# The low parts of the weights move from VectorE to GpSimd

## The chip, the cores and the metric

The kernel runs on one core of a Trainium2 chip. The metric is the device time of one execution in microseconds (us), as the median of the timed runs. The engines of the core are TensorE (PE, with its weight loads as PEld), VectorE (DVE), ScalarE (ACT), GpSimd (POOL) and SyncE (SP). Each runs its own program; they meet at semaphores.

## The reference

Two blocks of transformer-like layers run one after the other on one sequence of 512 tokens with 1024 channels, all in float32:

```python
def first_block(x, ...):
    for layer in range(DEPTH):                      # DEPTH = 2
        if layer % 2 == 0:
            x = x + even_mixer(rms_norm(x, even_norm[i]), even_w_in[i], even_w_out[i])
        else:
            x = x + diff_mixer(rms_norm(x, odd_norm[i]), odd_w_qkv[i], ...)
        x = x + conv_ffn(rms_norm(x, ffn_norm[layer]), ffn_w_up[layer], ..., ffn_w_down[layer])
    return rms_norm(x, final_norm)

def second_block(x, ...):
    for l in range(DEPTH):
        proj = x @ w_in[l]                          # retention, mLSTM and gates
        ...
        mix = (gate_a * y_ret + gate_b * y_ml) @ w_out[l]
        x = _layer_norm(DEEPNORM_ALPHA * x + mix, ln1_g[l], ln1_b[l])
        gu = x @ w_gate_up[l]
        hidden = jax.nn.silu(gu[..., :D_FF_2]) * gu[..., D_FF_2:]
        x = _layer_norm(DEEPNORM_ALPHA * x + hidden @ w_down[l], ln2_g[l], ln2_b[l])
    return x
```

Nearly all of the work is products of the activations with weight matrices. What matters here is that they must come out more exact than one pass of TensorE's fast float32 format (fp32r) gives.

## The kernel before

**Products in three passes.** Each weight w is split into a high part (w_hi, w rounded to fp32r) and a low part (w_lo = w - w_hi), and each activation likewise (h_hi, h_lo and others). A product is the sum of high by high, high by low and low by high, three matmuls of 512 columns for each weight tile of 128x128.

**Units.** The weights lie in memory as 512 units, in the order in which PE uses them. A unit is mostly 128x1024 float32 (four weight tiles of 256 columns, or two of 512); 16 units are half as large. A unit has 24 matmuls on PE. For each unit four engines do one thing: SP loads it into one of RAW = 3 raw buffers (w_raw); ACT makes w_hi in one of HL = 4 buffers; DVE makes w_lo in one of 4 buffers; PE multiplies. ACT waits until PE has finished the unit four before; SP waits until w_hi and w_lo of the unit three before are made, since they are read from the same raw buffer.

**Order.** There is no scheduler. Each engine's program is written out by hand and walks through the products in the same order with a class Panels, whose loops (fm for products with features in the rows, tm and tm_in_halves for products with tokens in the rows) call next_unit() wherever the next unit begins. On ACT and DVE next_unit() splits units up to HL ahead of the one that PE begins, so an engine's own work (copies, norms, attention) and the splits stand in one fixed order. On DVE the split of a unit is line L1423. Around it stand:

- L1546, L1817: h_lo of the norms. L1810, L1793: the layer norm's tiles; in layer_norm a call of next_unit() stands at the third tile.
- L1740, L1753, L1773, L1758: the convolution taps and the hidden tiles of the feed-forward blocks.
- L1598, L1626 (or L1623, L1624), L1633, L1725: the attention's score reduction with its row minimum, the normalising of probabilities, a copy of transposed probabilities, and a half of the copies of v out of PSUM. The other half is ACT's, L1098.

**Attention beside a product.** In both attentions of the first block the product for v (L574 on PE, tm_in_halves) is mixed with the steps of the first heads: scores (L640), transposes (L649), values (L660). This product uses two PSUM banks over and over, so it stops until DVE and ACT have copied v out. DVE's call there is `walk.tm_in_halves(beside_values(steps), late=True)`, which puts the unit's split behind the attention steps and ahead of the next copy of v.

**GpSimd before** (pool_program) does little: it starts table loads at certain points of the program, raises the head sums of the second attention to the power -0.5 (L2119), and helps with two tiles in the last norm (L2131, L2135).

**Once**: every wait goes through it; it leaves out a wait on a value that this engine has already seen.

Of the kernel before, what the change touches and what calls it, by code (L numbers as in the profile page):

```python
# [18 lines left out]
DT = D // P  # L19
TB = S // P  # L20
D_FF = 2816
FT = D_FF // P
# [96 lines left out]
RAW, HL = 3, 4  # L119
# [10 lines left out]
UNITS = weight_units()  # L130
# [1281 lines left out]
def dve_program(e, fl, m):  # L1412
    w = Once(e)
    mark, after, bank, scr, stats = fl.mark, fl.after, m.bank, m.scr, m.stats
    at = {"unit": 0, "split": 0}
    swapped = []

    def split_unit():
        u = at["split"]
        if u < N_UNITS:  # L1420
            n = UNITS[u][3] * UNITS[u][5]
            w.wait_ge(*after("w_hi", u))
            e.tensor_tensor(m.w_lo[u % HL][:, 0:n], m.raw[u % RAW][:, 0:n], f32(m.w_hi[u % HL][:, 0:n]),  # L1423
                            ALU.subtract).then_inc(*mark("w_lo", u))
            at["split"] += 1

    def next_unit():
        while at["split"] < min(at["unit"] + HL, N_UNITS):
            split_unit()
        at["unit"] += 1  # L1430

    walk = Panels(next_unit)
# [358 lines left out]
    def layer_norm(st, gain, shift, split):  # L1791
# [13 lines left out]
        for f in range(DT + 1 if split else ON_POOL):  # L1805
            if f == 2:
                next_unit()
            if f < DT:
                w.wait_ge(*after("recentred", (st, f)))
                e.scalar_tensor_tensor(m.x[:, f, :], m.x[:, f, :], m.p(gain, f), bank[SPREAD][:, :],  # L1810
                                       ALU.mult, ALU.mult).then_inc(*mark("x_normed", (st, f)))
            if f + ahead < (DT if split else ON_POOL):
                recentre(f + ahead)
            if f and split:
                g = f - 1
                w.wait_ge(*after("h_hi", (st, g)))
                e.scalar_tensor_tensor(m.h_lo[:, g, :], m.x[:, g, :], m.p(shift, g), f32(m.h_hi[:, g, :]),  # L1817
                                       ALU.add, ALU.subtract).then_inc(*mark("h_lo", (st, g)))
# [195 lines left out]
    split_unit()  # L2014
    w.wait_ge(*after("gains_in", 0))
    for f in range(DT):
        low_part("e", f, "even_norm")
        if f in (2, 4):
            split_unit()
    for f in range(1, DT):  # L2020
        tally_square("e", f)
        if f == 3:
            split_unit()
# [12 lines left out]
    for f in range(DT + 1):  # L2036
        if f == 2:
            next_unit()
# [55 lines left out]
def pool_program(e, fl, m, params, tables):  # L2094
    w = Once(e)
    mark, after, scr = fl.mark, fl.after, m.scr
    gains = PARAMS["subln"][0]

    w.wait_ge(*after(f"x_in{X_ON_SP - 1}", 0))
# [5 lines left out]
    for n, st in enumerate("ed"):  # L2105
# [3 lines left out]
        rows = [table(tables, "mask_rows")[:, i * S:(i + 1) * S] for i in range(2)]  # L2109
        w.wait_ge(*after("sumsq", (st, 7)))  # L2110
        if st == "e":
            e.dma_start(scr[4][:, :], rows[0]).then_inc(*mark("mask_rows_in", 0, by=16))
            e.dma_start(scr[5][:, :], rows[1]).then_inc(*mark("mask_rows_in", 1, by=16))
        else:
            e.dma_start(m.tally[:, :], rows[0]).then_inc(*mark("mask_rows_in", 2, by=16))
            for f0, f1 in HEAD_BATCHES.values():
                inv_head = m.stats[:, 128 + TB * f0:128 + TB * f1]
                w.wait_ge(*after("head_sums", f1 - 1))
                e.tensor_tensor(inv_head, inv_head, m.eps[:, 2:3].to_broadcast([P, TB * (f1 - f0)]), ALU.pow).then_inc(*mark("head_inv", f0))  # L2119
    for layer in range(DEPTH):  # L2120
# [4 lines left out]
            *mark("tables_in", ("rope", L), ("decay", L), by=16))  # L2125
        w.wait_ge(*after("headnorm", ("r" + L, NH2 * TB - 1)))
        e.dma_start(m.select, table(tables, "select")[0:NH2, :]).then_inc(*mark("tables_in", "select" + L, by=16))
    last = f"r{DEPTH}"
# [212 lines left out]
```

## Time and profile before

| what | value |
|---|---|
| timed runs | 3097.36 us median of 3 (3097.26 to 3099.04) |
| profiled execution, whole | 3099.19 us |
| its span | 3097.4 us |
| TensorE (PE) busy | 3069.8 us, 99% |
| VectorE (DVE) busy | 1611.7 us, 52% |
| ScalarE (ACT) busy | 1133.8 us, 37% |
| GpSimd (POOL) busy | 20.5 us, 1% |
| HBM traffic | 89 GB/s over the span |

A busy time is the sum of an engine's instructions in one profiled execution. A PE that counts as busy for 99% means that its matmuls overlap without a gap that the profile can see nearly all the time; it is a modelled end that closes small gaps. For the other engines it is what they work.

### The profile page before, as it was taken

Reading aid. Unit: us, or ns where it says so; the run is one execution under the profiler, and the core shown is the slowest. Engines: PE = TensorE matmul, PEld = TensorE weight load, DVE = VectorE, ACT = ScalarE, POOL = GpSimd, SP = SyncE. Lnnn points to the kernel's source line nnn. Section 1 sums busy time; section 2 is a strip of 40 time slices with the busy share of each in tenths; the row PEclk is TensorE's granted clock in tenths of the full one; section 3 lists DMA queues with packets and bytes.
Section 4 is the critical chain, followed back from the end, with each engine's and each line's share of the span. In section 5 each row is a group of like instructions: output and inputs, shape, how many; then the busy total and the mean of one; then the engine's idle time right before and its main releaser. Section 6 shows DMA issues by size and latency. Waiting matters only on the chain.

```text
span 3097.4 us, 35265 instructions
## 1 busy us (share of the span) xinstructions
PE 3069.8 (99%) x14003; PEld 2478.0 (80%) x14003; DVE 1611.7 (52%) x2498; ACT 1133.8 (37%) x1765; POOL 20.5 (1%) x27
## 2 busy tenths in 40 slices
PE   9999999999999999999999999999999999999998
PEld 7668888886688888887888888888887888888887
DVE  6766775366567753664424463334674424453324
ACT  3454443224544432344323343222454323333222
POOL 0000000000000000000000000000000000000000
PEclk9999999999999999999999999999999999999999
DMA  6312222242122232412232223323412232323321
GB/s 200 96 35 96 95 96 102 95 140 74 35 96 96 96 102 95 136 57 80 79 98 90 95 89 95 102 93 105 130 55 68 89 96 89 95 95 96 95 96 68
DMA packets 86531, 289.56 MB, mean 93 GB/s; under 512 B 11448, under 2 KB 11448, under 8 KB 86112
## 3 DMA queue, kind: packets, MB, share of 16 engines
q1 hardware_dynamic: 84016, 279.75, 28.4%
q0 software_dynamic: 1488, 6.22, 0.6%
q8 instruction: 112, 1.84, 0.2%
q10 hardware_dynamic: 864, 1.33, 0.1%
q14 instruction: 51, 0.42, 0.0%
HBM read 272.58 MB, written 2.10 MB: 89 GB/s over the span
## 4 chain that ended last, share of the span: by engine, by line
PE 95%; DVE 3%; ACT 1%; issue 1%; DMA 0%; ACTq 0%; DVEq 0%
PE banks L482 75%; PE banks L547 6%; PE banks L512 3%; PE banks L574 2%; PE banks L640 1%; PE banks L660 1%; PE banks L818 1%; PE banks L838 1%; PE banks L439 1%; PE banks L649 1%; PE banks L852 1%; PE banks L613 1%; PE banks L929 0%; DMA x_resid<-x_fm 0%; PE banks L803 0%
## 5 line engine op out<-in xcount | busy, mean ns | idle before, releaser
L1423 DVE TENSOR_TENSOR w_lo<-w_raw,w_hi 128x1024 fp32r<-128x1024 f32 (+1 forms) x512 | 612.2, 1207 | 880.8 <-ACT w_hi L969 879.8
L969 ACT ACTIVATE w_hi<-w_raw 128x1024 fp32r<-128x1024 f32 (+1 forms) x512 | 526.7, 1040 | 790.8 <-PE banks L482 729.8
L482 PE MATMUL banks<-h_hi,w_hi 128*128 128x512 f32 x2304 | 712.6, 390 | 0.5 <-ACT h_hi L1312 0.5
L482 PE MATMUL banks<-h_lo,w_hi 128*128 128x512 f32 x2304 | 709.7, 389 | 0.1
L482 PE MATMUL banks<-h_hi,w_lo 128*128 128x512 f32 x2304 | 709.3, 389 | 0.0
L482 PEld LDWEIGHTS banks<-h_lo,w_hi 128*128 128x128 f32 x2304 | 432.3, 188 | 90.9 <-DVE h_lo L1546 0.8
L482 PEld LDWEIGHTS banks<-h_hi,w_lo 128*128 128x128 f32 x2304 | 432.4, 188 | 90.0
L482 PEld LDWEIGHTS banks<-h_hi,w_hi 128*128 128x128 f32 x2304 | 430.3, 188 | 91.7 <-issue 2.8
L482 PE MATMUL banks<-hid_hi,w_hi 128*128 128x512 f32 x668 | 206.4, 390 | 0.0
L482 PE MATMUL banks<-hid_lo,w_hi 128*128 128x512 f32 x668 | 205.7, 389 | 0.0
L482 PE MATMUL banks<-hid_hi,w_lo 128*128 128x512 f32 x668 | 205.6, 389 | 0.0
L482 PEld LDWEIGHTS banks<-hid_hi,w_hi 128*128 128x128 f32 x668 | 125.4, 188 | 26.8 <-issue 1.0
L482 PEld LDWEIGHTS banks<-hid_hi,w_lo 128*128 128x128 f32 x668 | 125.4, 188 | 26.1
L482 PEld LDWEIGHTS banks<-hid_lo,w_hi 128*128 128x128 f32 x668 | 125.4, 188 | 26.1
L1112 ACT ACTIVATE scratch<-scratch,params_sb 128x512 f32<-128x512 f32 x88 | 67.0, 809 | 173.1 <-DVE scratch L1753 173.1
L1740 DVE SCALAR_TENSOR_TENSOR scratch<-scratch,params_sb,scratch 128x510 f32<-128x510 f32 (+1 forms) x176 | 122.4, 748 | 12.6 <-ACT scratch L1112 12.6
L1108 ACT ACTIVATE hid_hi<-scratch 128x512 fp32r<-128x512 f32 x88 | 54.3, 633 | 165.7 <-DVE scratch L1787 105.4
L1753 DVE TENSOR_TENSOR scratch<-banks,inverse_rms 128x512 f32<-128x512 f32 x88 | 56.7, 686 | 89.5 <-PE banks L482 80.2
L547 PE MATMUL banks<-w_hi,h_hi 128*128 128x512 f32 x256 | 82.7, 404 | 0.0
L547 PE MATMUL banks<-w_hi,h_lo 128*128 128x512 f32 x256 | 79.2, 390 | 0.0
L547 PE MATMUL banks<-w_lo,h_hi 128*128 128x512 f32 x256 | 78.9, 389 | 0.0
L482 PE MATMUL banks<-z_hi,w_lo 128*128 128x512 f32 x256 | 78.8, 389 | 0.0
(300 smaller groups left out, 3358.9 us busy)
## 6 DMA issues: line engine op xcount, KB each, us to landing
w_raw<-weights SPq DMA_DIRECT2D x496, 512.0 KB, 3.6
scratch<-scratch SPq DMA_DIRECT2D x128, 64.0 KB, 2.0
w_raw<-weights SPq DMA_DIRECT2D x16, 256.0 KB, 2.5
scratch<-scratch SPq DMA_DIRECT2D x32, 128.0 KB, 2.3
decay<-tables POOLq DMA_DIRECT2D x2, 1024.0 KB, 5.9
y_fm<-x_resid SPq DMA_DIRECT2D x8, 256.0 KB, 2.2
x_resid<-x_fm ACTq DMA_DIRECT2D x5, 256.0 KB, 8.0
rope<-tables POOLq DMA_DIRECT2D x2, 512.0 KB, 4.0
```

The lines of the kernel that those rows point to most:

```text
L439: mm = e.matmul(bank[b][:, tokens], wt[:, k, j * P:(j + 1) * P], a[:, kt + k, tokens], start=bool(j) and kt + k == kt0 and step == 0, stop ...
L482: mm = e.matmul(bank[b][:, :], wt[:, k, j * P:(j + 1) * P], a[:, kt, :], start=kt == 0 and step == 0, stop=step == 2 and (kt == k_tiles - ...
L512: mm = e.matmul(bank[b][:, :], weight[u % HL][:, :].rearrange("p (k c) -> p k c", k=4)[:, k, j * P:(j + 1) * P], a[:, kt, :], start=kt == ...
L547: mm = e.matmul(bank[t][:, :], a[:, kt, t * P:(t + 1) * P], wt[:, k, :], start=kt == 0 and step == 0, stop=kt == DT - 1 and step == 2)
L574: mm = e.matmul(bank[b][:, :], a[:, kt, t * P:(t + 1) * P], wt, start=kt == 0 and step == 0, stop=kt == DT - 1 and step == 2)
L613: mm = e.matmul(bank[b][:, tb * P:(tb + 1) * P], every_column(m.stats[:, first + tb:first + tb + 1]), m.ident[:, :], start=tb == 0, stop=T ...
L969: e.activation(m.w_hi[u % HL][:, 0:n], m.raw[u % RAW][:, 0:n], ACT.Copy).then_inc(*mark("w_hi", u))
L1108: e.activation(m.hid_hi[int(tag)][:, f, :], scr[2 + f % 2][:, :], ACT.Copy).then_inc(*mark("hid_hi", (tag, f)))
L1112: e.activation(scr[t][:, :], scr[4 + f % 2][:, :], ACT.Identity, bias=m.p("fconv_b" + tag, channels), scale=m.p("fconv_w" + tag, 2 * 2 * F ...
L1423: e.tensor_tensor(m.w_lo[u % HL][:, 0:n], m.raw[u % RAW][:, 0:n], f32(m.w_hi[u % HL][:, 0:n]), ALU.subtract).then_inc(*mark("w_lo", u))
L1740: c = e.scalar_tensor_tensor(scr[t][:, back:S], scr[u][:, 0:S - back], m.p("fconv_w" + tag, (2 - back) * 2 * FT + channels), scr[t][:, bac ...
L1753: e.tensor_tensor(scr[4 + f % 2][:, :], bank[b][:, :], m.r_bc[:, :], ALU.mult).then_inc(*mark(flow, (tag, f)))
```

## The change

The splits of all 512 units into low parts leave DVE's program and go to GpSimd's. DVE's walk keeps its loops, but with nothing to do where a unit begins. GpSimd gets a walk of its own, which passes through all the products in order with the helpers through and through_tm; its old work (table loads, head sums) stands between the stretches of that walk. The subtraction itself, its operands and its marks are the same. ACT, PE and SP are not changed, and PE and SP now wait for GpSimd's w_lo where they waited for DVE's.

```diff
 def dve_program(e, fl, m):
...
-    def split_unit():
-        u = at["split"]
-        if u < N_UNITS:
-            n = UNITS[u][3] * UNITS[u][5]
-            w.wait_ge(*after("w_hi", u))
-            e.tensor_tensor(m.w_lo[u % HL][:, 0:n], m.raw[u % RAW][:, 0:n], f32(m.w_hi[u % HL][:, 0:n]),
-                            ALU.subtract).then_inc(*mark("w_lo", u))
-            at["split"] += 1
-
-    def next_unit():
-        while at["split"] < min(at["unit"] + HL, N_UNITS):
-            split_unit()
-        at["unit"] += 1
-
-    walk = Panels(next_unit)
+    walk = Panels(lambda: None)
...
         for f in range(DT + 1 if split else ON_POOL):
-            if f == 2:
-                next_unit()
...
-    split_unit()
     w.wait_ge(*after("gains_in", 0))
     for f in range(DT):
         low_part("e", f, "even_norm")
-        if f in (2, 4):
-            split_unit()
...
 def pool_program(e, fl, m, params, tables):
...
+    at = {"unit": 0, "split": 0}
+
+    def split_unit():
...
+    def next_unit():
...
+    walk = Panels(next_unit)
+
+    def through(tiles, k_tiles):
+        for _ in walk.fm(tiles, k_tiles):
+            pass
+
+    def through_tm():
+        for _ in walk.tm(iter(())):
+            pass
+
+    for _ in range(2):
+        split_unit()
     w.wait_ge(*after(f"x_in{X_ON_SP - 1}", 0))
     e.dma_start(m.ones[:, :], table(tables, "ones")).then_inc(*mark("small_in", 0, by=16))
...
+        next_panel = walk.fm(DT, DT)
+        next(next_panel)
         w.wait_ge(*after("sumsq", (st, 7)))
...
+        for _ in next_panel:
+            pass
+        through(DT, DT)
+        through_tm()
+        if st == "d":
             for f0, f1 in HEAD_BATCHES.values():
                 inv_head = m.stats[:, 128 + TB * f0:128 + TB * f1]
                 w.wait_ge(*after("head_sums", f1 - 1))
                 e.tensor_tensor(inv_head, inv_head, m.eps[:, 2:3].to_broadcast([P, TB * (f1 - f0)]), ALU.pow).then_inc(*mark("head_inv", f0))
+        through(DT, DT)
+        through(2 * FT, DT)
+        through(DT, FT)
...
+        through(DT, DT)
+        through_tm()
+        through(DT, DT)
         w.wait_ge(*after("headnorm", ("r" + L, NH2 * TB - 1)))
         e.dma_start(m.select, table(tables, "select")[0:NH2, :]).then_inc(*mark("tables_in", "select" + L, by=16))
+        through_tm()
+        for _ in range(7):
+            through(DT, DT)
+        through(2 * FT, DT)
+        through(DT, FT)
```

The first place is DVE's program beside the v product of the second attention, at the second of its four copies of v. Before, a low part stands ahead of the copy of v (L1725):

```order
L1598 ISA prob_d,stats<-banks,diagonals 128x256
L1598 ISA stats 128x1
L1633 COPY probt_d<-banks 128x384
L1626 SCALAR_TENSOR_TENSOR prob_d<-prob_d,stats 128x256
L1423 TENSOR_TENSOR w_lo_61<-w_raw_54,w_hi_57 128x1024
L1725 TENSOR_SCALAR v_d<-banks,stats 128x512
L1598 ISA prob_d,stats<-banks,diagonals 128x128
```

With the change the same piece reads (line numbers are 16 lower):

```order
L1582 ISA prob_d,stats<-banks,diagonals 128x256
L1582 ISA stats 128x1
L1617 COPY probt_d<-banks 128x384
L1610 SCALAR_TENSOR_TENSOR prob_d<-prob_d,stats 128x256
L1709 TENSOR_SCALAR v_d<-banks,stats 128x512
L1582 ISA prob_d,stats<-banks,diagonals 128x128
```

The copy of v has moved up behind the normalising of the probabilities; the rest is as it was. The same happens wherever L1423 stood, 512 times.

The second place is the beginning of GpSimd's program. Before, it goes from the memsets to the loads of tables:

```order
L2100 DMA ones<-tables 128x128
L2101 DMA ident<-tables 128x128
L2102 DMA eps<-tables 128x3
L2103 DMA params_sb<-params 128x1369
L2104 DMA masks_f_77<-tables 128x768
L2108 DMA rope_e<-tables 128x1024
L2112 DMA scratch_73<-tables 128x512
```

With the change (the numbers tell the buffers of a ring apart):

```order
L2080 ISA
L2080 TENSOR_TENSOR w_lo_59<-w_raw_52,w_hi_55 128x1024
L2080 TENSOR_TENSOR w_lo_60<-w_raw_53,w_hi_56 128x1024
L2102 DMA ones<-tables 128x128
L2103 DMA ident<-tables 128x128
L2104 DMA eps<-tables 128x3
L2105 DMA params_sb<-params 128x1369
L2106 DMA masks_f_77<-tables 128x768
L2110 DMA rope_e<-tables 128x1024
L2080 TENSOR_TENSOR w_lo_61<-w_raw_54,w_hi_57 128x1024
L2080 TENSOR_TENSOR w_lo_62<-w_raw_52,w_hi_58 128x1024
L2080 TENSOR_TENSOR w_lo_59<-w_raw_53,w_hi_55 128x1024
```

Two low parts now stand ahead of the first table loads and three behind them, and the ISA row, which before stood ahead of L2119, has come to the front.

## Rows read from the trace of the kernel before

**Rows 1.** The page: busy time of engines, and the chain that ended last.

```profile
PE 3069.8 (99%) x14003; PEld 2478.0 (80%) x14003; DVE 1611.7 (52%) x2498; ACT 1133.8 (37%) x1765; POOL 20.5 (1%) x27
...
PE 95%; DVE 3%; ACT 1%; issue 1%; DMA 0%; ACTq 0%; DVEq 0%
```

**Rows 2.** Windows; columns are window, its length, then busy time by engine.

```profile
core 0: us, PE busy (x) PEld busy (x) DVE busy (x) ACT busy (x) POOL busy (x), PEclk, DMA share, GB/s
99.00:216.00 117.00, 114.78 (x610) 67.11 (x609) 86.76 (x271) 65.36 (x181) 0.00 (x0) 1.00 0.16 47
709.00:834.00 125.00, 116.66 (x579) 76.62 (x578) 80.30 (x248) 66.80 (x178) 5.23 (x3) 0.99 0.15 44
216.00:627.00 411.00, 411.00 (x1826) 340.69 (x1826) 238.37 (x301) 159.49 (x205) 0.53 (x1) 1.00 0.29 96
...
815.60:819.00 3.40, 3.40 (x13) 2.69 (x14) 1.51 (x3) 0.40 (x1) 0.00 (x0) 0.50 0.00 0
```

**Rows 3.** The page's groups of instructions: busy us, mean ns, idle before.

```profile
L1423 DVE TENSOR_TENSOR w_lo<-w_raw,w_hi 128x1024 fp32r<-128x1024 f32 (+1 forms) x512 | 612.2, 1207 | 880.8 <-ACT w_hi L969 879.8
```

**Rows 4.** Timeline of GpSimd at the end: start, duration of the row.

```profile
3087.39 2.49 POOL L2131 TENSOR_TENSOR x_resid<-x_resid,inverse_rms 128x512 f32<-128x512 f32 x2 [800.28 <-ACT inverse_rms L1202]
```

**Rows 5.** Timeline of ACT, DVE and PE in the first feed-forward block.

```profile
485.24 1.99 ACT L969 ACTIVATE w_hi<-w_raw 128x1024 fp32r<-128x1024 f32 x2
486.31 2.36 DVE L1423 TENSOR_TENSOR w_lo<-w_raw,w_hi 128x1024 fp32r<-128x1024 f32 x2 [0.26 <-ACT w_hi L969]
495.22 0.61 PE L482 MATMUL banks<-h_hi,w_hi 128*128 128x512 f32 x2
```

**Rows 6.** The page's DMA issues: KB each, us from issue to landing.

```profile
w_raw<-weights SPq DMA_DIRECT2D x496, 512.0 KB, 3.6
x_resid<-x_fm ACTq DMA_DIRECT2D x5, 256.0 KB, 8.0
```

**Rows 7.** Timeline of DVE, ACT and PE behind a layer norm.

```profile
1801.39 1.22 DVE L1423 TENSOR_TENSOR w_lo<-w_raw,w_hi 128x1024 fp32r<-128x1024 f32 x1
1813.53 2.00 ACT L969 ACTIVATE w_hi<-w_raw 128x1024 fp32r<-128x1024 f32 x2
1816.51 0.62 PE L512 MATMUL banks<-h_hi,w_hi 128*128 128x512 f32 x2
```

**Rows 8.** Timeline of DVE and PE in the first attention.

```profile
129.57 1.22 DVE L1423 TENSOR_TENSOR w_lo<-w_raw,w_hi 128x1024 fp32r<-128x1024 f32 x1
131.88 0.70 PE L640 MATMUL banks<-k_e,q_e 64*128 64x256 f32 x4 [0.25 <-DVE stats L1598]
```

**Rows 9.** Timeline of DVE, ACT and PE in the second attention, 743 to 747.

```profile
743.65 0.47 DVE L1626 SCALAR_TENSOR_TENSOR prob_d<-prob_d,stats 128x256 f32<-128x256 f32 x1
744.04 1.22 DVE L1423 TENSOR_TENSOR w_lo<-w_raw,w_hi 128x1024 fp32r<-128x1024 f32 x1
745.18 0.74 DVE L1725 TENSOR_SCALAR v_d<-banks,stats 128x512 f32<-128x512 f32 x1
...
744.75 0.67 ACT L1098 ACTIVATE v_d<-banks,stats 128x512 f32<-128x512 f32 x1
...
746.07 0.70 PE L574 MATMUL banks<-w_hi,h_hi 128*128 128x512 f32 x2 [1.01 <-DVE v_d L1725]
```

**Rows 10.** Timeline of DVE and PE in the second attention, 793 to 796.

```profile
793.13 1.22 DVE L1423 TENSOR_TENSOR w_lo<-w_raw,w_hi 128x1024 fp32r<-128x1024 f32 x1 [3.58 <-ACT w_hi L969]
795.08 0.92 PE L640 MATMUL banks<-k_d,q_d 64*128 64x384 f32 x4 [0.69 <-DVE v_d L1725]
```

**Rows 11.** Timeline of DVE, PE and its weight loads at the start.

```profile
6.34 1.23 DVE L1423 TENSOR_TENSOR w_lo<-w_raw,w_hi 128x1024 fp32r<-128x1024 f32 x1 [5.06 <-ACT w_hi L969]
8.74 0.63 PE L482 MATMUL banks<-h_hi,w_lo 128*128 128x512 f32 x2
17.69 0.30 PEld L482 LDWEIGHTS banks<-h_lo,w_hi 128*128 128x128 f32 x2 [0.55 <-DVE h_lo L1546]
```

**Rows 12.** Timeline of GpSimd and DVE in the second attention, about 800.

```profile
799.21 2.29 POOL L2119 TENSOR_TENSOR stats<-stats,eps 128x12 f32<-128x12 f32 x1 [171.65 <-DVE stats L1645]
800.20 0.48 DVE L1626 SCALAR_TENSOR_TENSOR prob_d<-prob_d,stats 128x256 f32<-128x256 f32 x1
```

More of the change, by code:

```diff
@@ L1414, in dve_program @@
     mark, after, bank, scr, stats = fl.mark, fl.after, m.bank, m.scr, m.stats
-    at = {"unit": 0, "split": 0}
     swapped = []
-    def split_unit():
-        u = at["split"]
-        if u < N_UNITS:
-            n = UNITS[u][3] * UNITS[u][5]
-            w.wait_ge(*after("w_hi", u))
-            e.tensor_tensor(m.w_lo[u % HL][:, 0:n], m.raw[u % RAW][:, 0:n], f32(m.w_hi[u % HL][:, 0:n]),
-                            ALU.subtract).then_inc(*mark("w_lo", u))
-            at["split"] += 1
-    def next_unit():
-        while at["split"] < min(at["unit"] + HL, N_UNITS):
-            split_unit()
-        at["unit"] += 1
-    walk = Panels(next_unit)
+    walk = Panels(lambda: None)
     def inverse_root(st):
@@ L2017, in dve_program @@
         low_part("e", f, "even_norm")
-        if f in (2, 4):
-            split_unit()
     for f in range(1, DT):
         tally_square("e", f)
-        if f == 3:
-            split_unit()
     w.wait_ge(*after("small_in", 2))
@@ L2036, in dve_program @@
     for f in range(DT + 1):
-        if f == 2:
-            next_unit()
         if f < DT:
@@ L2097, in pool_program @@
     gains = PARAMS["subln"][0]
+    at = {"unit": 0, "split": 0}
+    def split_unit():
+        u = at["split"]
+        if u < N_UNITS:
+            n = UNITS[u][3] * UNITS[u][5]
+            w.wait_ge(*after("w_hi", u))
+            e.tensor_tensor(m.w_lo[u % HL][:, 0:n], m.raw[u % RAW][:, 0:n], f32(m.w_hi[u % HL][:, 0:n]),
+                            ALU.subtract).then_inc(*mark("w_lo", u))
+            at["split"] += 1
+    def next_unit():
+        while at["split"] < min(at["unit"] + HL, N_UNITS):
+            split_unit()
+        at["unit"] += 1
+    walk = Panels(next_unit)
[6 more added lines that the diff above has]
+    for _ in range(2):
+        split_unit()
     w.wait_ge(*after(f"x_in{X_ON_SP - 1}", 0))
```

## The prediction

> **What bounds the kernel now.** I read the page's busy shares first: TensorE (PE) is busy for 3069.8 us of a span of 3097.4, VectorE (DVE) for 1611.7, GpSimd (POOL) for 20.5 [rows 1]. The chain that ended last gives PE 95% and DVE 3% [rows 1]. So a change of DVE's work can only move the time where PE stands waiting for DVE, or where PE is made to wait for something new. All the idle time of PE in the trace is 3097.4 - 3069.8 = 27.6 us.
>
> Second, the table of windows: where is that idle time? In the long products it is nil: from 216 to 627 us PE is busy for 411.00 of 411 [rows 2]. In the first attention (99 to 216) it is 117 - 114.78 = 2.2 us, in the second (709 to 834) 125 - 116.66 = 8.3 us [rows 2]. The rest is the start, the last 20 us and a few us around the norms.
>
> Third, the groups of DVE: the low parts of the weights are 512 instructions, 612.2 us in all, 1207 ns in the mean [rows 3], 38% of DVE's busy time. In the timeline one of 1024 columns takes 1.22 us; 16 of the 512 have 512 columns. They leave DVE altogether.
>
> **What the change costs on GpSimd.** No row shows GpSimd subtracting 1024 columns. The nearest are its operations on 128x512 f32 with two SBUF inputs at the end: two in a row take 2.49 us, 1.245 us each [rows 4]. Between half of a doubling, were a large part of it fixed, and a full doubling, 1024 columns cost 1.3 to 2.5 us; I take the full 2.46, since it is the same operation on twice the columns. GpSimd's sum is 496 x 2.46 + 16 x 1.23 = 1240 us, 40% of the span, and a unit has 24 matmuls, which at 411 us for 1826 [rows 2] is 5.4 us of PE. On average it keeps up by a factor of two.
>
> **Dense stages: nothing.** What counts is not the average but when each low part is due. In the first feed-forward block two high parts start at 485.24, DVE's subtractions run from 486.31 (2.36 us for two), and PE reaches the first of these units at 495.22 [rows 5]. On GpSimd the first low part ends at 486.31 + 2.46 = 488.8, the second at 491.2, due at 500.6: 6.4 and 9.4 us to spare. PE's work hides the edit; without this cover each would cost 1.24. The raw tile is also freed 1.2 us later for the first and 2.5 for the second; a load lands 3.6 us after its issue [rows 6], so the next raw tile is there by about 495, and ACT, which has its own work, turned to the next pair of high parts only about then. That is the tightest hand-over of the ring, and a high part a microsecond late still has those 6 us.
>
> The tightest due times are behind the norms. At 1813.53 ACT makes the high part of the fourth unit of an up projection, because it stands behind eight tiles of h_hi; PE wants it at 1816.51 [rows 7]. GpSimd would end at 1814.57 + 2.46 = 1817.0, which is 0.5 us late. But DVE's own w_lo at 1801.39 (1.22 us) stands in the middle of the row of norm tiles that feeds ACT [rows 7]. It is gone, so all tiles behind it and that high part come 1.22 us earlier, and GpSimd ends at 1815.8, with 0.7 to spare, just as DVE did. The same holds at the two other places of the kind. Sum here: 0, at worst 3 x 0.5 = 1.5 us.
>
> The tables that GpSimd loads between units come late by at most two low parts and a high part, about 6 us by the prices above; between each such load and its first use lie two units of products or more, 11 us. Cost 0. Where GpSimd's program stands behind a wait for head sums in the second attention, it has already split three units of the next product, 16 us of PE, and the last wait ends as that product begins. Cost 0.
>
> **Attention: the gain.** Here DVE's order matters, because PE takes a few scores, then a few value products, and waits for DVE to free a bank. Three places show a low part straight ahead of what PE waits for:
> - PE waits 0.25 us at 131.88 for DVE, which came 1.22 us late out of the w_lo of 129.57 [rows 8].
> - PE waits 1.01 us at 746.07 for v_d, which follows the w_lo of 744.04 [rows 9]. ACT must empty the other bank too, and does so only shortly before; I count 0.65.
> - PE waits 0.69 us at 795.08 for v_d, which stands behind the w_lo of 793.13. DVE had been idle for 3.58 us before it, for the sake of that unit's high part alone [rows 10]. Count 0.69.
>
> Sum 1.6 us. The other idle time in the second attention stands behind ACT copies and head sums without a low part on the way, so the change does not touch it. In 815.6 to 819 the granted clock is 0.50 [rows 2]; PE had been idle for much of the four microseconds before. I expect it again, since nothing on that piece moves.
>
> **Start: about nothing.** w_lo of unit 0 began at 6.34 on DVE, as soon as its high part was there, and PE wants it at 8.74 [rows 11]. On GpSimd it ends at 6.3 + 2.46 = 8.8: 0.1 us. PE then waits for x tiles and h_lo anyway, 0.55 us at 17.69 in the weight load [rows 11], where DVE no longer has three low parts between the h_lo. I take 0 (from -0.5 to +0.5). The order shows one more row: an ISA row ahead of GpSimd's first tensor_tensor, which I take for the loading of its code. Before, it stood where GpSimd idled for 171.65 us [rows 12]; now it stands at the very start. The rows bound it only by 0 and by what a 256 KB transfer of the first microseconds takes, 8.0 us to landing [rows 6]: then w_lo 0 would end at about 11 instead of 8.8, most of it made up while PE waits for x, so 0 to 1.5 us. The Trainium skill (GPSIMD Engine Reference, Instruction dispatch) says of a freshly loaded kernel's first call that it pays about 6 us; by that the code would be there at about 6.5, and the sum would stay the same.
>
> **Sum.** 3099.19 (the profiled execution's own time) - 1.6 = 3097.6. That execution was 1.8 us above the median of the timed runs, 3097.36; the same step from the median gives 3095.8, and that is what I predict. A measurement of this kernel can tell about 0.2%, 6.2 us, from no change. This is a fourth of it.
>
> **Rivals.** *Turn-taking between DVE and GpSimd.* Most of DVE's instructions beside the weights read two SBUF tiles, as GpSimd's subtraction does. If they exclude each other, DVE stands for up to 2.46 us behind each low part where it was busy for 1.22: 1.24 us worse instead of 1.22 better. For it: nothing in this kernel has ever run GpSimd over long tiles while DVE reads two. Against it: from 799.21 to 801.50 GpSimd runs a tensor_tensor, and DVE's L1626, two SBUF inputs, starts in the middle of it, at 800.20, and takes 0.48 us [rows 12], where the same shape took 0.47 at 743.65 [rows 9]; but GpSimd read only 12 columns there. The Trainium skill (SBUF — State Buffer, Who interferes with whom) has it as a rule: two SBUF inputs on VectorE contend with a GpSimd instruction that reads SBUF, and one blocks the other for its whole length. The row shows no such block for the whole length, and cannot show one for long reads. In dense stages 6 us of spare time swallow it. In the attentions 16 low parts stand beside value products: if PE had no slack at any, 16 x 1.24 = 19.8 us, 3117. It decides from five such places (6.2 us). Going through them, most have a microsecond or two of slack, and with turn-taking I come to v_d of 746 and one score bank at 126 about 0.6 later each, 0.3 lost at the start, the first and third gain kept: 2 x 0.6 + 0.3 - 0.25 - 0.69 = +0.6, 3098, still no measurable change. Chance that it becomes slower by this: 0.11.
>
> *GpSimd becomes the bound.* Needs a low part of over 5.4 us, 2.2 times my price. At 6 us the time would be about 3097 + 512 x 0.6 = 3400. Chance 0.02.
>
> *The code load or the table loads hold up the start*, by 6 us or more: 3104. Chance 0.03.
>
> *More gain*: all idle time in both attentions goes, 10.5 us: 3087. The chain of these waits speaks against it. Chance 0.06.
>
> **Chances and range.** Forecast (no change that can be measured, light turn-taking included) 0.78; faster 0.06; slower 0.11 + 0.02 + 0.03 = 0.16. The range goes from 3091.5 (all of the second attention's DVE waits, and the start) to 3106 (seven bad places in attention, or the start); beyond lie about 0.05 below and 0.1 above.
>
> **What would show it.** L2080 on GpSimd at 2.4 to 2.5 us x496, POOL busy near 1250, DVE near 1000; PE idle before v_d at 746 and 795 gone; no PE wait in the table of waits for a w_lo; PE still at 411 of 411 in the block behind the first attention. Turn-taking would show as DVE instructions with two SBUF inputs (L1626, L1740, L1758, whose numbers fall by 16) that start late or take longer wherever an L2080 runs, or as L2080 above 2.5. The prediction is wrong if PE's rows in the products show gaps named after w_lo.

## The result, and the profile after

The changed kernel takes 3106.12 us (median of 14 runs, 3104.32 to 3108.49); the kernel before, beside it, 3098.89 us (14 runs, 3097.26 to 3100.29). The ratio is 1.0023 with a 95% interval of 1.0016 to 1.003: it is slower, by 7.2 us, just beyond what I had called measurable, and outside my range. The two profiled spans say the same, 3104.2 against 3097.4: 6.8 us to find.

The page of the kernel after, its busy times and its last chain, answering to [rows 1]:

```profile
PE 3070.9 (99%) x13999; PEld 2479.8 (80%) x14003; DVE 1152.8 (37%) x1986; ACT 1132.9 (36%) x1765; POOL 1243.6 (40%) x539
...
PE 92%; DVE 5%; ACT 2%; issue 1%; DMA 0%; ACTq 0%; DVEq 0%
```

The clue stands in the first line. The low parts took 612.2 us from DVE [rows 3], so 1611.7 - 612.2 = 999.5 should be left. DVE shows 1152.8. Its remaining instructions have grown by 153 us, and DVE's share of the chain went from 3% to 5%.

Which ones grew? Groups of the kernel after, by shape (busy us, mean ns, idle before). The first is GpSimd's, the others DVE's:

```profile
L2080 POOL TENSOR_TENSOR w_lo<-w_raw,w_hi 128x1024 fp32r<-128x1024 f32 x496 | 1202.5, 2430 | 1764.7 <-ACT w_hi L969 1763.2
...
L1724 DVE SCALAR_TENSOR_TENSOR scratch<-scratch,params_sb,scratch 128x511 f32<-128x511 f32 x88 | 64.2, 751 | 12.7 <-ACT scratch L1112 12.7
L1737 DVE TENSOR_TENSOR scratch<-banks,inverse_rms 128x512 f32<-128x512 f32 x88 | 56.7, 686 | 234.1 <-PE banks L482 220.7 <-ACT inverse_rms L994 13.3
...
L1936 DVE SCALAR_TENSOR_TENSOR scratch<-scratch,params_sb,scratch 128x511 f32<-128x511 f32 x16 | 23.1, 1485 | 25.6 <-ACT scratch L1379 25.6
L1530 DVE SCALAR_TENSOR_TENSOR h_lo<-x_resid,params_sb,h_hi 128x512 fp32r<-128x512 f32 x32 | 28.2, 918 | 11.3 <-ACT h_hi L1312 8.9 <-ACT h_hi L1006 2.4
L1474 DVE TENSOR_TENSOR diagonals<-x_resid 128x512 f32<-128x512 f32 x8 | 15.9, 1984 | 0.3
L1906 DVE TENSOR_SCALAR ml_tm<-ml_tm,stats 128x256 f32<-128x256 f32 x32 | 18.8, 667 | 0.1
```

In the kernel before the last four had means of 747, 749, 692 and 417 ns. All four have only SBUF operands. L1737 reads a PSUM bank and kept its 686 ns, although about half of its 88 instructions ran beside a low part. L1724, two SBUF tiles, kept its 751 too: its order in the feed-forward blocks never puts it beside a low part.

The timelines show what "grown" means. The start, DVE, PE and GpSimd (start, duration, in brackets the idle time before):

```profile
12.01 2.40 POOL L2080 TENSOR_TENSOR w_lo<-w_raw,w_hi 128x1024 fp32r<-128x1024 f32 x1 [3.22 <-ACT w_hi L969]
12.78 2.84 DVE L1530 SCALAR_TENSOR_TENSOR h_lo<-x_resid,params_sb,h_hi 128x512 fp32r<-128x512 f32 x2 [1.01 <-ACT h_hi L1312]
15.01 0.73 PE L482 MATMUL banks<-h_lo,w_hi 128*128 128x512 f32 x2 [1.02 <-DVE h_lo L1530]
15.88 5.49 DVE L1530 SCALAR_TENSOR_TENSOR h_lo<-x_resid,params_sb,h_hi 128x512 fp32r<-128x512 f32 x3 [0.26 <-ACT h_hi L1312]
17.73 2.42 POOL L2080 TENSOR_TENSOR w_lo<-w_raw,w_hi 128x1024 fp32r<-128x1024 f32 x1
20.77 0.73 PE L482 MATMUL banks<-h_lo,w_hi 128*128 128x512 f32 x2 [1.38 <-DVE h_lo L1530]
```

An h_lo that is issued while a low part runs ends 0.55 us after that low part ends, as if it had begun only then, and its whole wait is booked as its duration: the first of the two at 12.78 takes 2.18 us instead of 0.75. One h_lo even waits for a low part whose row has not begun. It is the second of the three at 15.88: it starts at 16.55, 1.2 us before the low part of 17.73, lasts 4.16 us, and ends 0.55 us after that low part. GpSimd was issuing table loads in between. The same loads held nothing up in e2 below, where no low part of GpSimd follows them (0.75 us each), and why the wait reaches back so far is not shown. PE waits twice for an h_lo, 1.02 and 1.38 us, the second time for this one. This is the turn-taking of my rival: where the two meet, VectorE's instruction stands until GpSimd's has ended.

Around a layer norm of the second block, DVE and PE:

```profile
1780.52 4.70 DVE L1462 TENSOR_TENSOR x_resid<-x_resid,inverse_rms 128x512 f32<-128x512 f32 x4 [2.71 <-ACT inverse_rms L1155]
...
1788.86 1.59 DVE L1474 TENSOR_TENSOR diagonals<-x_resid 128x512 f32<-128x512 f32 x1
1790.37 3.86 DVE L1481 TENSOR_TENSOR scratch<-scratch,scratch 128x512 f32<-128x512 f32 x5
1794.15 0.68 DVE L1455 TENSOR_TENSOR x_resid<-x_resid,banks 128x512 f32<-128x512 f32 x1
...
1797.74 0.66 PE L602 MATMUL banks<-ones,diagonals 128*128 128x64 f32 x4 [1.40 <-DVE diagonals L1496]
1799.90 3.43 PE L613 MATMUL banks<-ident,stats 128*128 128x128 f32 x16
```

The same place in the kernel before:

```profile
1777.56 2.50 DVE L1478 TENSOR_TENSOR x_resid<-x_resid,inverse_rms 128x512 f32<-128x512 f32 x4 [3.06 <-ACT inverse_rms L1155]
...
1793.76 0.66 PE L602 MATMUL banks<-ones,diagonals 128*128 128x64 f32 x4 [0.38 <-DVE diagonals L1512]
...
1795.93 2.12 PE L613 MATMUL banks<-ident,stats 128*128 128x128 f32 x16
```

The loss arises at L1462: one of its four tiles meets the low part of 1781.52, and the four take 4.70 us instead of 2.50. Only one low part of 1.22 us has left DVE's row up to there, so DVE is 1.0 us late. L1474 takes 1.59 us instead of 0.69, but behind it another low part of 1.22 has gone, and this meeting costs nothing more. So DVE reaches the last tiles 1.0 us later relative to PE, and PE's wait ahead of L602 is 1.40 us (0.38 before). Then the 16 transposes of L613 take 3.43 us instead of 2.12: the granted clock fell here to 0.50, the lower of its two levels (1.2 of 2.4 GHz). Windows (columns as in [rows 2]):

```profile
216.00:627.00 411.00, 411.00 (x1830) 339.73 (x1829) 149.22 (x225) 158.18 (x204) 177.32 (x77) 1.00 0.31 95
1801.00:1803.00 2.00, 2.00 (x11) 2.00 (x11) 0.69 (x1) 0.54 (x1) 1.38 (x1) 0.50 0.00 0
```

At the two gated convolutions of the second block the wait reaches PE through ACT:

```profile
1395.96 4.76 POOL L2080 TENSOR_TENSOR w_lo<-w_raw,w_hi 128x1024 fp32r<-128x1024 f32 x2 [5.55 <-ACT w_hi L969]
1398.53 6.04 DVE L1936 SCALAR_TENSOR_TENSOR scratch<-scratch,params_sb,scratch 128x511 f32<-128x511 f32 x6 [4.26 <-ACT scratch L1379]
1403.94 1.29 ACT L1383 ACTIVATE mqk<-scratch 128x512 f32<-128x512 f32 x2 [4.74 <-DVE scratch L1936]
1405.14 1.99 ACT L969 ACTIVATE w_hi<-w_raw 128x1024 fp32r<-128x1024 f32 x2
1407.04 1.06 ACT L1374 ACTIVATE scratch<-banks 128x512 f32<-128x512 f32 x2
1407.66 0.98 PE L547 MATMUL banks<-w_hi,h_hi 128*128 128x512 f32 x2 [0.71 <-ACT scratch L1374]
```

The first of the six taps (L1936) waits for the second low part, so that the six take 6.04 us where they took 4.10. ACT's program has the next high parts and the emptying of a bank (L1374) behind them, so each round of two units lasts 10.3 us (w_hi at 1384.53, then at 1394.84) where it could last 8.4 (1381.10 to 1389.47). At the end of the second such round PE stands, for 0.71 us in the last line. That these taps are the cause of PE's delay is tested in e10.

In the first attention the normalising of probabilities (L1607, one SBUF tile) does it:

```profile
135.71 2.38 POOL L2080 TENSOR_TENSOR w_lo<-w_raw,w_hi 128x1024 fp32r<-128x1024 f32 x1 [3.52 <-ACT w_hi L969]
135.90 2.35 DVE L1607 TENSOR_SCALAR prob_e<-prob_e,stats 128x256 f32<-128x256 f32 x1
138.43 0.74 DVE L1709 TENSOR_SCALAR v_e<-banks,stats 128x512 f32<-128x512 f32 x1
139.31 0.70 PE L574 MATMUL banks<-w_hi,h_hi 128*128 128x512 f32 x2 [1.00 <-DVE v_e L1709]
```

The gains came too: the waits of [rows 9, 10] are 0.29 us at 748.25 (1.01 before) and none at 795.18, where v_d now starts as soon as PE's bank is full.

To add it up, I compared the start of each matmul in the two timelines. PE's lag behind the kernel before, in us, and its step:

| place (us of before) | step | lag after it |
|---|---|---|
| 14 to 20, h_lo at the start | +1.69 | 1.69 |
| 125.9, score bank | +0.57 | 2.26 |
| 131.9, [rows 8] | -0.18 | 2.08 |
| 136.4, v_e | +0.87 | 2.95 |
| 746.1, [rows 9] | -0.44 | 2.51 |
| 795.1, [rows 10] | -0.71 | 1.80 |
| 1405.1, gated convolution | +1.15 | 2.94 |
| 1793.8, layer norm | +1.03 | 3.97 |
| 1796.5, granted clock 0.50, small changes to 2171 | +0.83 | 4.80 |
| 2326.1, gated convolution | +1.18 | 5.98 |
| 2714.7, layer norm | +0.82 | 6.80 |

The losses are 8.1 us, the gains 1.3. The long products between these places add nothing.

### The profile page after: what moved, and what is told of

It reads as the page before. It is cut to its first block, busy times and chain, and to the rows that moved or that the text cites. A ratio compares the mean times of both kernels' runs of the same rounds, so it can differ in the third digit from the quotient of the medians.

```text
span 3104.2 us, 35261 instructions
## 1 busy us (share of the span) xinstructions
PE 3070.9 (99%) x13999; PEld 2479.8 (80%) x14003; DVE 1152.8 (37%) x1986; ACT 1132.9 (36%) x1765; POOL 1243.6 (40%) x539
## 4 chain that ended last, share of the span: by engine, by line
PE 92%; DVE 5%; ACT 2%; issue 1%; DMA 0%; ACTq 0%; DVEq 0%
PE banks L482 72%; PE banks L547 6%; PE banks L512 3%; PE banks L574 2%; PE banks L640 1%; PE banks L660 1%; DVE scratch L1936 1%; PE banks L818 1%; PE banks L838 1%; PE banks L439 1%; PE banks L649 1%; PE banks L613 1%; PE banks L852 1%; PE banks L929 0%; ACT w_hi L969 0%
## 5 line engine op out<-in xcount | busy, mean ns | idle before, releaser
L2080 POOL TENSOR_TENSOR w_lo<-w_raw,w_hi 128x1024 fp32r<-128x1024 f32 (+1 forms) x512 | 1223.4, 2395 | 1799.3 <-ACT w_hi L969 1797.8
L1771 DVE TENSOR_TENSOR scratch<-banks,scratch 128x512 f32<-128x512 f32 x44 | 28.4, 686 | 398.8 <-PE banks L482 381.5
L1737 DVE TENSOR_TENSOR scratch<-banks,inverse_rms 128x512 f32<-128x512 f32 x88 | 56.7, 686 | 234.1 <-PE banks L482 220.7
L1724 DVE SCALAR_TENSOR_TENSOR scratch<-scratch,params_sb,scratch 128x510 f32<-128x510 f32 (+1 forms) x176 | 122.3, 748 | 12.7 <-ACT scratch L1112 12.7
L1442 DVE TENSOR_TENSOR x_resid<-x_resid,banks 128x512 f32<-128x512 f32 x31 | 20.0, 684 | 233.4 <-PE banks L482 230.0
```

The source lines that it names most:

```text
L1724: c = e.scalar_tensor_tensor(scr[t][:, back:S], scr[u][:, 0:S - back], m.p("fconv_w" + tag, (2 - back) * 2 * FT + channels), scr[t][:, bac ...
L1737: e.tensor_tensor(scr[4 + f % 2][:, :], bank[b][:, :], m.r_bc[:, :], ALU.mult).then_inc(*mark(flow, (tag, f)))
```

## The experiments

Theory A: exclusion between VectorE's SBUF-only instructions and GpSimd's low part. Theory B: a slowdown by GpSimd's load or traffic, spread over the program. Theory C: the longer low part hands over w_lo and the raw tile late. The intervals of the ratios are about 0.0009 wide on either side, 2.8 us. By their times alone e2, e3 and e8 can't be told from the change, nor e4, e9 and e11 from the kernel before; there the timelines decide. In seven of the runs below both engines walk through all units, and a set decides which of them splits a unit:

```diff
+ON_DVE = {...}
+def low_flow(u):
+    return "w_lo_dve" if u in ON_DVE else "w_lo"
...
-            w.wait_ge(*after("w_lo", u))
+            w.wait_ge(*after(low_flow(u), u))
```

**e1, the places of loss back on VectorE**

```diff
+ON_DVE = {*range(5), *range(20, 24), *range(219, 227), *range(375, 383), *range(287, 291), *range(443, 447)}
```

> The changed kernel, but the low parts of 37 of the 512 units are back on VectorE, at the places where the comparison of the two traces shows PE falling behind: units 0 to 4 (start), 20 to 23 (first attention), 219 to 226 and 375 to 382 (convolution behind the retention gates), 287 to 290 and 443 to 446 (layer norms). Theory A, exclusion: a VectorE instruction whose operands all lie in SBUF waits for the whole of a GpSimd low part that is running; then the losses of these places (1.7 + 0.6 + 0.9 + 1.15 + 2.1 + 1.2 + 0.8 = 8.4 us) go and the gains of the second attention (0.44 and 0.71) stay: span near 3096.3, 1.1 below the kernel before, time ratio 0.9996. Theory B, a general slowdown spread over the program by GpSimd's traffic (475 of 512 low parts still run there): span near 3103.5, 0.3 us given back of 6.8. Theory C, GpSimd's longer low part frees the raw tiles late and the loads come late: the same as A at these places, but then waits for DMA or w_hi must show at the others, and DVE's instructions keep their lengths.

Span 3097.5; 3099.35 against 3098.59 us, ratio 1.0002 (0.9993 to 1.0011). With 475 of 512 low parts still on GpSimd the loss is gone, which rules out B. C asked that DVE's instructions keep their lengths, and in the change they did not. The span is 1.2 us more than A says, and the trace names why, and here C does have a part: PE is 0.76 us later at 1816 and at 2737, with a wait on a low part. The wait and its cause (PE and GpSimd):

```profile
1813.36 4.76 POOL L2112 TENSOR_TENSOR w_lo<-w_raw,w_hi 128x1024 fp32r<-128x1024 f32 x2 [45.88 <-ACT w_hi L976]
1815.91 0.70 PE L519 MATMUL banks<-h_hi,w_hi 128*128 128x512 f32 x2 [0.51 <-POOL w_lo L2112]
```

Unit 290 stands on DVE in the row of norm tiles, unit 291 comes whole on GpSimd: the very case that my prediction priced at 0.5 us and excluded, because in the real change the low part of 1801.39 [rows 7] leaves DVE as well.

**e2, only the start on VectorE** (`ON_DVE = set(range(5))`)

> The changed kernel with only units 0 to 4 on VectorE. Theory A: the h_lo (L1530 of the changed kernel, 1.76, 2.18 and 4.16 us long at the start) fall back to 0.75 each, PE gains 1.7 us at the start and keeps the rest of the loss: span near 3102.5. If instead GpSimd's first call (loading of its code) costs the start, that call now comes at the sixth unit, where some 5 us are spare, and the span is 3102.5 too, but the h_lo would not have been long; theory B: 3104.

Span 3100.9 and ratio 1.0018 (1.0009 to 1.0027). The h_lo took 0.75 us each, and PE was 0.1 us ahead at 100 us, not 1.7 behind: that step is right. The span is 1.6 us below what A said, and that is the clock: its fall at 815 to 819 did not happen (PE gained 1.66 there), and the one of 1800 appeared at 2718.6 instead. This profiled execution was a quick one of its kernel, 3102.73 us where the median is 3104.33.

**e3, only the layer norms on VectorE** (`ON_DVE = {*range(287, 291), *range(443, 447)}`)

> The changed kernel with only units 287 to 290 and 443 to 446, the ones around the first layer norm of each layer of the second block, on VectorE. Theory A: L1474 and L1481 no longer wait for a low part, PE's wait before L602 falls from 1.4 to 0.4 us at both places, and the fall of the granted clock to 0.50 at 1800 to 1804, which followed a PE idle for 1.4 us, does not happen: span 3104.2 - 1.0 - 1.1 - 0.8 = 3101.3. If the clock's fall has nothing to do with that wait it stays: 3102.4. Theory B: 3104.

Span 3102.9, ratio 1.002 (1.0011 to 1.0029). Both steps at L602 are gone and so is the fall of the clock at 1800. (That PE's wait of 1.4 us caused that fall is not shown: in the changed kernel the same 1.40 us ahead of L602 at 2721.77 had no fall behind it.) Of the 1.6 us above 3101.3, 1.5 are e1's waits for units 291 and 447, 0.76 and 0.77 here.

**e4, only three low parts on GpSimd** (`ON_DVE = set(range(512)) - {21, 122, 126}`)

> The kernel before, but with the low parts of three units (21, 122 and 126, those that stood ahead of what PE waited for at 131.88, 746.07 and 795.08) on GpSimd and 509 on VectorE. By my prediction's own prices the three waits go: 0.25 + 0.65 + 0.69 = 1.6 us. The trace of the changed kernel showed 0.18, 0.44 and 0.71: span near 3096.1, a time ratio of 0.9996. A theory in which GpSimd's low part costs as much at these places as it gives: 3097.4 or more.

Span 3095.6, 1.8 less than before. PE's steps are -0.45, -0.88 and -0.74, and it arrives at the last norm 2.1 us earlier; 0.3 are lost in the last ten microseconds. The time, 3097.37 against 3098.59 us, gives 0.9997 (0.9988 to 1.0006): too small for the measurement, as foretold.

**e5, which forms are excluded**

```diff
+        if u in range(36, 92):
+            w.wait_ge(*after("w_hi", u))
+            e.memset(m.probe[0][:, :], 0.0)
+            for i in (1, 2):
+                ...    # one of seven forms, eight units each, 128x256 f32 in SBUF
```

> The changed kernel (all low parts on GpSimd) with probes on VectorE, which is nearly idle in the first feed-forward block: for each of the units 36 to 91 it waits for the same high part as GpSimd's low part and then runs a memset of 192 columns and two instructions of one form on 128x256 f32 in SBUF, eight units for each of seven forms: tensor_tensor of two tiles, tensor_copy, tensor_scalar with an immediate, tensor_scalar with a scalar per partition, reciprocal, memset, bn_stats. Nothing else depends on them. Theory A (an instruction with two reads from SBUF excludes GpSimd's): the first form lasts up to 2.4 us, the others 0.3 to 0.4. Theory A' (all that touches SBUF alone is excluded): all seven last up to 2.4 us. From the rows of the changed kernel (ml_tm by tensor_scalar of one tile took 2.49 us beside a low part, RECIPROCAL of 4 columns 0.18) I expect forms 1 to 4 to wait, and reciprocal, memset and bn_stats not. The time says nothing; span within 3 us of 3104.

Means of the 16 instructions of each form (DVE):

```profile
L1445 DVE RECIPROCAL probe<-params_sb 128x256 f32<-128x256 f32 x16 | 26.4, 1695 | 0.0
L1443 DVE TENSOR_SCALAR probe<-params_sb,eps 128x256 f32<-128x256 f32 x16 | 22.9, 1471 | 0.0
L1437 DVE TENSOR_TENSOR probe<-params_sb 128x256 f32<-128x256 f32 x16 | 22.1, 1423 | 0.0
L1439 DVE COPY probe<-params_sb 128x256 f32<-128x256 f32 x16 | 19.6, 1269 | 0.0
L1441 DVE TENSOR_SCALAR probe<-params_sb 128x256 f32<-128x256 f32 x16 | 19.6, 1268 | 0.0
L1433 DVE MEMSET probe<- 128x192 f32 x56 | 12.2, 218 | 61.4 <-ACT w_hi L977 57.7 <-DVE probe L1443 0.7 <-DVE probe L1439 0.7
L1449 DVE BATCH_NORM_STATS2 probe<-params_sb 128x6 f32<-128x256 f32 x16 | 5.5, 387 | 0.0
L1447 DVE MEMSET probe<- 128x256 f32 x16 | 4.4, 272 | 0.0
```

The means of the four forms mix two values: two-tile, copy and both tensor_scalar forms last 0.2 to 0.4 us alone and 2.1 to 2.6 where they meet a low part. These are the forms 1 to 4 that I expected to wait. Reciprocal only looks long: each of its 16 took 1.69 or 1.70 us, beside a low part or not. It, memset and bn_stats are free of it. The Trainium skill (SBUF — State Buffer, Who interferes with whom) states just this split: two SBUF inputs contend with a GpSimd instruction that reads SBUF, copy, cast and tensor_scalar in their two-port modes contend, other instructions with at most one SBUF input don't. The trace agrees for each form that was tried. The span, 3131.0 in the one execution there is, was far from the 3104 that I expected. It shows that a product stage is not immune: with some 5 us of probes for each two units PE waited 17.5 us in all for w_lo, up to 2.9 at a time.

**e6 and e7, what GpSimd does to exclude**

```diff
-            e.tensor_tensor(m.w_lo[u % HL][:, 0:n], m.raw[u % RAW][:, 0:n], f32(m.w_hi[u % HL][:, 0:n]),
-                            ALU.subtract).then_inc(*mark("w_lo", u))
+            e.memset(f32(m.w_lo[u % HL][:, 0:n]), 0.0).then_inc(*mark("w_lo", u))      # e6
+            e.tensor_copy(m.w_lo[u % HL][:, 0:n], m.raw[u % RAW][:, 0:n]).then_inc(*mark("w_lo", u))      # e7
```

> The changed kernel with GpSimd writing zeros to each w_lo (memset of the same 1024 columns, same waits and marks) in place of the subtraction; the low parts of the weights are left out of the result. GpSimd then writes SBUF and reads nothing. If the exclusion hangs on GpSimd's reads, VectorE's instructions fall back to the durations of the kernel before, the seven losses go and the gains stay: span near 3095.6. If it hangs on GpSimd using its port at all, VectorE waits as long as a memset lasts, and with a memset of 1 us or more a part of the losses stays: 3097 to 3104.

> The changed kernel with GpSimd copying w_raw to w_lo (one read from SBUF instead of two) in place of the subtraction; the low parts then hold the weights themselves, so the result is another. If two reads of GpSimd are needed for the exclusion: span near 3095.6 and no long instructions on VectorE. If one read is enough: VectorE's two-tile instructions last up to the length of the copy plus 0.55 us, and the span stands between 3097 and 3104 by the copy's length (1.2 us would give about half of the losses: 3100).

The same DVE group, tally of the norm, with e6's memset and then with e7's copy:

```profile
L2080 POOL MEMSET w_lo<- 128x1024 f32 x496 | 473.9, 956 | 2461.2 <-ACT w_hi L969 2461.1
...
L1474 DVE TENSOR_TENSOR diagonals<-x_resid 128x512 f32<-128x512 f32 x8 | 5.5, 692 | 0.3
```

```profile
L2080 POOL CAST w_lo<-w_raw 128x1024 fp32r<-128x1024 f32 x496 | 521.3, 1058 | 2416.3 <-ACT w_hi L969 2416.3
...
L1474 DVE TENSOR_TENSOR diagonals<-x_resid 128x512 f32<-128x512 f32 x8 | 8.6, 1070 | 0.3
```

They are almost equally long, 956 and 1058 ns, but beside the memset the two-tile instruction keeps its 692 ns and takes 1.45 us where it began while a copy ran. One read by GpSimd is enough, and a write alone is not, for two-tile instructions. For tensor_scalar a write is enough: in e6 the ml_tm of 0.41 us took 1.13 to 1.28 at four places where a memset ran. Spans: 3094.0 (ratio 0.9985, 0.9976 to 0.9995) and 3094.9 (0.9989, 0.998 to 0.9999). A low part that cost only what a copy costs would have made the change a small gain, of 0.1%. My guess of 3100 for e7 was wrong: the loss does not go with the length in proportion. A meeting costs a two-tile instruction at most 1.45 - 0.69 = 0.76 us there, less than the 1.22 that left VectorE, so at most places nothing is lost; that is argued from these rows and not tested by itself. e6 is 1.6 us quicker than I said, in spite of a second fall of the clock at 1240. PE gained more in the attentions than from the three waits of the prediction: its step at 744 is -1.3 us where it was -0.4 in the change.

**e8, halves**

```diff
+            for c, done in ((0, False), (n // 2, True)):
+                part = e.tensor_tensor(m.w_lo[u % HL][:, c:c + n // 2], ...)
```

> The changed kernel with each low part as two instructions of 512 columns (w_lo is marked by the second); 1.25 to 1.3 us each. Theory A with whole instructions taking turns: a single VectorE instruction waits at most 1.3 us instead of 2.4, so the start gives back about 0.8 us and the first attention about 0.7; a row of VectorE instructions, as in the convolution and before the norms, now waits for two halves one after the other and gains nothing. Span near 3102.5. If instead VectorE only loses what GpSimd's traffic takes (a share of bandwidth), nothing changes: 3104.2 or a little more, since GpSimd works 50 us longer.

Span 3101.6, ratio 1.0014 (1.0004 to 1.0023). The start gives back all of its 1.7 us by 22 us (0.5 come again at 33). The row of taps gains nothing:

```profile
L1936 DVE SCALAR_TENSOR_TENSOR scratch<-scratch,params_sb,scratch 128x511 f32<-128x511 f32 x16 | 23.5, 1508 | 25.6 <-ACT scratch L1379 25.6
```

The mean is 1508 ns against 1485 with whole low parts (now the first two taps of a row wait 1.0 us each, before the first waited 2.0), and PE's steps at the convolutions (1.05, 1.03) and norms (1.18, 1.17) stay. The attention's place at 136 did not gain either (0.81), contrary to what I expected. The second attention did gain, by a step of -1.3 at 744 instead of -0.4, which I had not expected either and did not follow up. Here too the clock changed its places: no fall at 815, others at 1241 and 1797. B would have given 3104.2 or more.

**e9, the places mended**

```diff
+ON_DVE = {*range(5), 20, 22, 23, *range(219, 227), *range(375, 383), *range(287, 292), *range(443, 448)}
```

> As the first experiment (the low parts at the places of loss on VectorE, the rest on GpSimd), mended where its trace showed what was left: units 291 and 447, whose low parts PE waited for (0.76 us each at 1816 and 2737, since unit 290 or 446 stood ahead on VectorE and the whole low part behind on GpSimd), are on VectorE too, and unit 21 is on GpSimd for the gain at 131.88. If those readings are right: span 3097.5 - 1.5 - 0.4 = 3095.6, and no wait of PE for w_lo; 463 of 512 low parts then lie on GpSimd at no cost, and the time stands where the kernel with only three of them there stands. If something else holds the 1.5 us: 3097.1.

Span 3095.6, no wait of PE for a w_lo; 3096.81 against 3098.58 us, 0.9993 (0.9984 to 1.0002). The reading of e1 was right. This and e4 are the best versions that still compute everything, 1.8 us of span better than before and 8.6 better than the change, but no measurable gain on the kernel before.

**e10 and e11, one part of the change alone** (`ON_DVE = set(range(512)) - {*range(219, 227), *range(375, 383)}` and `set(range(5, 512))`)

> The kernel before with only one part of the change: the 16 low parts beside the two gated convolutions (units 219 to 226 and 375 to 382) on GpSimd, 496 on VectorE. Exclusion: the first tap of every pair lasts 2.7 us again and PE loses 1.15 and 1.18 us at L547, span 3097.4 + 2.3 = 3099.7, as large a loss with 16 low parts moved as with 512. If the loss came from the load of the whole (GpSimd at 40%), these 16 cost nothing: 3097.4.

> The kernel before with only units 0 to 4 on GpSimd. Exclusion: h_lo of the first x tiles last 2.2 to 4.2 us, PE is 1.7 us later by 21 us, and nothing behind it is changed: span 3099.1. The granted clock fell once at 815 in the kernel before and in most others, but not in the one where the start alone was given back; if that fall is moved or doubled here, the span is another 1.3 to 1.7 us off in either direction, which the clock's rows will show.

Spans 3100.3 (ratio 1.0011, 1.0002 to 1.002) and 3099.2 (1.0007, 0.9998 to 1.0016). PE's steps at the convolutions are +1.17 and +1.19 with 16 low parts moved, as with all 512; the start alone gives +1.76. PE arrives at the last norm of e10 2.1 us late; the rest of its 2.9 lies in the last ten microseconds. The losses are made place by place and add up. I had said 3099.7 and 3099.1.

## Why the prediction was wrong

**What bounds the kernel**: right. Only PE's waits matter, and the long products still show 411 of 411.

**GpSimd's price**: 2.46 predicted, 2.40 measured (the mean is 2.43 with what it waits for DVE itself); the sum of the low parts 1240 predicted, 1223 measured (1243.6 is all of GpSimd's work). GpSimd as the bound: no.

**Dense stages, nothing**: right in the change as made. Its reason, 6 us to spare, was too general, as e5 shows.

**Behind the norms, 0 for the low part that PE wants**: right. No wait of PE on PE's own timeline is named after w_lo (its weight load has one, 0.56 us at 8.84, which delays nothing beyond the 0.1 us foretold), and e1 and e3 measured the excluded case (0.5 predicted, 0.76 by PE's step). The slack was smaller than said: the high part came 0.9 us earlier relative to PE, not 1.22, and the low part was ready about 0.35 us ahead of PE, not 0.7. But I had looked only at when the low part is due, not at what it does to the DVE tiles ahead of the norm. That is where 1.03 and 0.82 us were lost.

**Attention gain 1.6**: mechanism right. 0.18 + 0.44 + 0.71 = 1.3 in the change, 2.1 where the three low parts move alone (e4).

**Start, -0.5 to +0.5**: wrong, 1.7. Not through the load of code: the first low part began at 6.43, 0.1 us after its high part, and ended at 8.79, as foretold (8.8). The six microseconds that the Trainium skill gives for a first call (GPSIMD Engine Reference, Instruction dispatch) did not show as a wait here; whether they lie in the 5.97 us in which GpSimd waited for the first high part, no row tells. It was the h_lo.

**Turn-taking, nothing in the sum, +0.6 as a rival with a chance of 0.11**: this is the step that failed. The runs show 7.3 us of losses by it at seven places, and with the clock's second fall 8.1. The mechanism was named, with its sign and almost its price for one place (1.24 us; the measured waits are mostly up to 2.2, once 3.4, less the 1.22 that left). Three things went wrong in the sizing:
- I took the row of [rows 12] as evidence against it. GpSimd had 12 columns to read there and showed 2.29 us; it says nothing on 1024. The changed kernel has both cases for one instruction: L1610 on 128x128 takes 0.35 us at 802.56 beside that operation of GpSimd, and 1.40 at 748.44 beside a low part.
- I let it act in the attentions alone. Of the 8.1 us lost, 1.4 lie in the attentions, 1.7 at the start, 2.3 at the gated convolutions, 1.9 at the layer norms and 0.8 in the clock. The convolution (L1954 before) appears nowhere in my text: PE waited for nothing there, so I did not look at how much slack its round of ACT and DVE had.
- Against the rule that the Trainium skill states outright (SBUF — State Buffer, Who interferes with whom) I set one row of another size. With the rule taken at its word, each group of DVE with SBUF operands alone had to be followed through every stage with w_lo beside it.

**The clock**: I expected the fall at 815 again, and it came. A second one at 1800 was not foreseen.

## What to carry to other kernels

Before moving work to GpSimd, list VectorE's instructions whose operands are all in SBUF and find where they will meet it: each meeting costs the rest of GpSimd's instruction, here up to 2.2 us with few exceptions. Instructions with a PSUM source, reciprocal, bn_stats and memset did not wait in these runs. In a trace the wait looks like a longer instruction, not like idle time, so compare mean durations by shape. Look for the places with a closed loop of engines (VectorE to ScalarE to TensorE and back), even where TensorE waits for nothing yet; and move single instructions where a wait names them instead of a whole kind.

## What the runs showed of the hardware

- The hand-over goes by whole instructions, and in the rows below it alternates. At 1371.73 a scan of DVE (1.21 us alone) waits for the first of two low parts, 3.11 us in all; then the second low part waits for the scan and lasts 3.31 us, as one other does, the longest of all 512; then DVE's next instruction (0.68 alone) waits 2 us:

```profile
1371.37 5.68 POOL L2080 TENSOR_TENSOR w_lo<-w_raw,w_hi 128x1024 fp32r<-128x1024 f32 x2 [33.35 <-ACT w_hi L969]
1371.73 3.11 DVE L1920 TENSOR_TENSOR_SCAN row<-row,row 4x512 f32<-4x512 f32 x1
1374.88 2.71 DVE L1923 TENSOR_TENSOR row<-row,row 4x512 f32<-4x512 f32 x1
```

  In e8 it goes the same way: the first tap waits for the first half, the second tap for the second half. This is why halves do not help a row of taps.
- GpSimd's plain copy of 1024 columns takes 1.06 us and its subtraction of two tiles 2.40, so the columns alone are not what is dear. The second operand and the arithmetic were not separated.
- The granted clock's falls to 0.50 took 3.4 us each and came at a few places: about 815, 1240, 1800 and 2718, in e5 also at 496 and 524. At 815, 1800 and 2718 PE had idled for 1.5 us or more in the four microseconds before, and in e5 for 2.9 us, waiting for w_lo. At 1240 (e6, e7 and e8) it had idled for only 0.2. At which of these places a fall comes differs between kernels that differ by a microsecond or two ahead of it. The kernel before and e9 had one before the last twenty microseconds, the changed kernel two. One costs 1.3 to 1.7 us, so spans that differ by less than that can differ by the clock alone. What triggers them was not tested and stays open.
